# Weight sums of the seven-product pairs made in block zero and split when read; block one on seven products too

## What is computed

```python
h = rmsnorm(x, g_pre)
proj = h @ w_in                       # 1024 x 10240: twelve parts of 512 columns, then 4 x 1024 gate columns
out_a, out_b, out_c, out_d = ...      # chunk mixing | 31-tap conv | pooling | 3-tap conv, each times silu(z)
merged = sum(sigmoid(gate_i + b_i) * (out_i @ w_branch[i]) for i in range(4))
y = merged @ w_out
x = x + rmsnorm(y, g_post)
```

## Time and profile before

| | |
|---|---|
| median of 3 runs | 2377.5 us (2376.88 to 2377.93) |
| profiled execution | 2379.08 us, span 2377.0 us |
| mean granted TensorE clock | 0.998 |
| TensorE matmul busy | 2356.2 us, 99% |
| VectorE, ScalarE, GpSimd busy | 1568.0, 442.9, 633.1 us |
| DMA | 686.63 MB, mean 289 GB/s |

### The profile page before, as it was taken

One profiled execution on the slowest core, in us unless ns is written; L12 is line 12 of the kernel. 1 busy time (PEld: TensorE's weight loads), 2 busy tenths in 40 slices (PEclk: granted clock), 3 DMA queues, 4 the chain that ended last, 5 costly groups with the idle time before them and its releaser, 6 DMA issues.

```text
span 2377.0 us, 34997 instructions
## 1 busy us (share of the span) xinstructions
PE 2356.2 (99%) x13240; PEld 2086.9 (88%) x13240; DVE 1568.0 (66%) x2347; ACT 442.9 (19%) x646; POOL 633.1 (27%) x423
## 2 busy tenths in 40 slices
PE   9999999999999999999999999999999999999998
PEld 7888888888788888788888899999898999999998
DVE  7886887855666577775266866776337776577643
ACT  5223222323112111122101100111110110010111
POOL 4435545455545646656200000000100000000000
PEclk9999999999999999999999999999999999999999
DMA  8977878788998998999765599999875458988884
GB/s 329 321 249 278 308 261 326 271 296 329 376 326 288 364 328 321 371 325 363 292 252 186 204 322 374 306 331 323 271 252 163 157 186 287 332 281 267 282 284 173
DMA packets 286115, 686.63 MB, mean 289 GB/s; under 512 B 19665, under 2 KB 97873, under 8 KB 258577
## 3 DMA queue, kind: packets, MB, share of 16 engines
q1 hardware_dynamic: 273520, 652.18, 78.3%
q10 hardware_dynamic: 12448, 32.49, 3.6%
HBM read 514.14 MB, written 170.46 MB: 288 GB/s over the span
## 4 chain that ended last, share of the span: by engine, by line
PE 88%; DVE 5%; issue 2%; POOL 1%; POOLq 1%; DMA 1%; DVEq 1%; ACT 1%; SPq 0%; ACTq 0%
PE acc L1928 47%; PE acc L2146 18%; PE side L2157 7%; PE side L2072 4%; PE side L2146 4%; PE acc L2306 3%; PE side L2306 3%; POOL s_lo L669 1%; DMA w_pair<-split_main 1%; PE acc L2303 1%; PE side L2303 1%; PE side L2100 1%; PE side L2090 1%; DVE t_sum L1413 0%; PE acc L2336 0%
## 5 line engine op out<-in xcount | busy, mean ns | idle before, releaser
L1928 PE MATMUL acc<-h_hi,w_pair 128*128 128x512 f32 x2752 | 866.2, 390 | 6.4 <-DMA w_pair<-split_main 6.2
L1928 PEld LDWEIGHTS acc<-h_hi,w_pair 128*128 128x128 f32 x2752 | 517.4, 188 | 116.2 <-issue 7.7
L1928 PE MATMUL acc<-h_lo,w_pair 128*128 128x512 f32 x1376 | 536.1, 390 | 0.0
L1200 DVE SCALAR_TENSOR_TENSOR cb<-glu,col,cb 128x512 f32<-128x512 f32 x600 | 425.0, 773 | 18.9 <-issue 10.9
L648 POOL TENSOR_TENSOR w_pair<-w_raw,w_pair 128x1024 fp32r<-128x1024 f32 x118 | 268.4, 2286 | 273.1 <-ACT w_pair L779 258.1
L678 POOL TENSOR_TENSOR rstd<-msq,nhalf 128x5 f32<-128x5 f32 (+4 forms) x19 | 19.9, 1047 | 1126.7 <-DVE msq L1110 532.3
L1928 PEld LDWEIGHTS acc<-h_lo,w_pair 128*128 128x128 f32 x1376 | 258.6, 188 | 53.4
L2146 PE MATMUL acc<-t_hi,chunk 128*128 128x256 f32 (+1 forms) x1344 | 266.8, 287 | 1.3 <-DVE merged L1505 1.3
L2146 PEld LDWEIGHTS acc<-t_hi,chunk 128*128 128x128 f32 x1344 | 216.6, 189 | 2.0 <-DVE merged L1505 1.7
L2146 PE MATMUL acc<-h_hi,chunk 128*128 128x256 f32 (+1 forms) x1008 | 205.1, 289 | 2.6 <-issue 1.5
L2146 PE MATMUL acc<-t_lo,chunk 128*128 128x256 f32 (+1 forms) x672 | 193.0, 287 | 0.0
(11 more groups left out here) (327 smaller groups left out, 3405.6 us busy)
## 6 DMA issues: line engine op xcount, KB each, us to landing
w_pair<-split_main SPq DMA_DIRECT2D x118, 1024.0 KB, 7.2
chunk<-split_main SPq DMA_DIRECT2D x226, 512.0 KB, 5.8
chunk<-s_parts SPq DMA_DIRECT2D x200, 512.0 KB, 6.2
split_main<-w_pair SPq DMA_DIRECT2D x88, 1024.0 KB, 6.7
w_raw<-in_w_main SPq DMA_DIRECT2D x88, 512.0 KB, 5.1
chunk<-split_branch SPq DMA_DIRECT2D x62, 512.0 KB, 4.5
s_raw<-in_w_main SPq DMA_DIRECT2D x100, 256.0 KB, 6.0
s_parts<-s_hi SPq DMA_DIRECT2D x50, 512.0 KB, 5.2
```

What stands on the lines that cost most here:

```text
L1200: dve.scalar_tensor_tensor(dst, src, c1("conv_w", c * CK + t), dst, ALU.mult, ALU.add)
L1928: ins = pe.matmul(acc[:, s, b, 0:m], w_k[:, wt, wk], mv_[:, k, t0:t0 + m], start=(k == 0 and n == 0), stop=(k == nk - 1 and n == 2))
```

## The change

SEVEN0 becomes 1: block one does its 25 pairs with seven products as blocks two and three do. The weight sums are made in block zero by GpSimd, from the raw tiles while both units of a pair lie in the ring, just before the low part of the pair's second unit. A pair's units are f and f + 2 in the G sections (f + 1 and f + 3 are branch tiles) and f and f + 1 in D and Z. The sums are stored unsplit (1 MB for a pair instead of 2) from one buffer, and the raw tile of either unit is held until they are made. When a sum chunk is read, it is 256 KB; ScalarE casts it (chunk_cast) and GpSimd subtracts (chunk_low). The loops of SP and GpSimd over block zero's units are written out. A small buffer for the sample rows (x_dec) is cut in four pieces, since s_sum takes its place.

```diff
-SEVEN0 = 2
+SEVEN0 = 1
+SUM_AT = (1, 2, 3, 5)
@@ SBUF and DRAM
-    s_parts = nc.dram_tensor("s_parts", (NPAIR, P, 2, 4 * WB), F32).ap()
+    chunk_raw = [sb(f"chunk_raw{c}", [P, WB], addr=pair_at + (c * 2 + 1) * WB * 4) for c in range(CHUNKS)]
+    s_parts = nc.dram_tensor("s_parts", (NPAIR, P, 4, WB), F32).ap()
+    s_sum = sb("s_sum", [P, 4, WB], addr=a + 2 * WMAX * 4 + EL * 4)
@@ SP, raw_load(u, src, n)
+            if u >= RING:
                 sp.wait_ge(w_lo_done, u - RING + 1)
+                if u - RING in PAIR_OF:
+                    sp.wait_ge(s_summed, SUM_RANK[PAIR_OF[u - RING]] + 1)
+            sp.dma_start(w_raw[u % RING][:, 0:n], src).then_inc(w_landed[u % RING], 16)
@@ SP, split_store(u)
+            sp.dma_start(dst, src).then_inc(split_stored[u % RING], 16)
+            if second:
+                sp.wait_ge(s_summed, SUM_RANK[p] + 1)
+                sp.dma_start(s_parts[p, :, :, :], s_sum[:, :, :]).then_inc(s_stored, 16)
@@ SP, for every unit u of block zero
+                        raw_load(u, raw_rows(m), DM)
+                if u >= RING:
+                    split_store(u - RING)
@@ SP, blocks after
-                        for h in range(NH):
-                            if HALF_STORE[h] == u // 2:
-                                s_store(h)
...
-                                s_load(h)
+            dst = chunk_raw[n % CHUNKS][:, :] if STREAM[n][0] == "sum" else f(chunk[n % CHUNKS])
+            sp.dma_start(dst, chunk_source(*STREAM[n])).then_inc(chunk_landed[n % CHUNKS], 16)
@@ GpSimd
+        def lo(u, n):
             pool.wait_ge(w_hi_done, u + 1)
+            s, p = u % RING, PAIR_OF.get(u)
+            if p is not None and u == PAIR_UNITS[p][1]:
+                pair_weights(p)
             pool.tensor_tensor(w_lo[s][:, 0:n], w_raw[s][:, 0:n], f(w_hi[s])[:, 0:n],
                                ALU.subtract).then_inc(w_lo_done, 1)
+        def pair_weights(p):
...
+            s1, s2, s3, s4 = (s_sum[:, c, :] for c in range(4))
+            if SUM_RANK[p]:
+                pool.wait_ge(s_stored, 16 * SUM_RANK[p])
+            pool.tensor_tensor(s3, a21, a11, ALU.subtract)
             pool.drain()
+            pool.tensor_tensor(s1, a22, a21, ALU.add)
+            pool.tensor_tensor(s2, a22, s3, ALU.add)
             pool.drain()
+            pool.tensor_tensor(s4, a12, s2, ALU.subtract)
             pool.drain().then_inc(s_summed, 1)
+        def chunk_low(j, p, at):
+
+            n = PAIR_AT[j, p][0] + at
+            pool.wait_ge(c_hi_done, sum_no(j, p, at) + 1)
+            pool.tensor_tensor(chunk[n % CHUNKS][:, 1, :], chunk_raw[n % CHUNKS][:, :], f(chunk[n % CHUNKS])[:, 0, :],
+                               ALU.subtract).then_inc(c_lo_done, 1)
@@ ScalarE
+        def chunk_cast(j, p, at):
+
+            n = PAIR_AT[j, p][0] + at
+            act.wait_ge(chunk_landed[n % CHUNKS], 16 * (n // CHUNKS) + 16)
+            act.activation(chunk[n % CHUNKS][:, 0, :], chunk_raw[n % CHUNKS][:, :], ACT.Copy).then_inc(c_hi_done, 1)
@@ ScalarE, seven_pairs
                 copy_p1(j, p)
+                chunk_cast(j, p, SUM_AT[3])
+                if p + 1 < NPAIR:
+                    chunk_cast(j, p + 1, SUM_AT[0])
+                    chunk_cast(j, p + 1, SUM_AT[1])
+                    if name == "D":
+                        chunk_cast(j, p + 1, SUM_AT[2])
...
+                        if t == 0 and p + 1 < NPAIR:
+                            chunk_cast(j, p + 1, SUM_AT[2])
@@ TensorE, product
+                if summed is None:
+                    landed(n)
+                else:
+                    pe.wait_ge(c_lo_done, summed + 1)
```

More of the change, by code:

```diff
@@ L420, in gp, with sum_no @@
         return (j - SEVEN0) * NPAIR + p
+    def sum_no(j, p, at):
+        return 4 * gp(j, p) + SUM_AT.index(at)
     def chunk_no(j, p):
@@ L572, in s_store @@
-        def s_store(h):
-            q, hx, b = h // 2, h % 2, h % 3
-            sp.wait_ge(s_lo_done, h + 1)
-            for n, part in enumerate((s_hi[b], s_lo[b])):
-                dst = s_parts[q, :, n, :].rearrange("p (c n) -> p c n", c=8)
-                sp.dma_start(dst[:, hx::2, :], f(part)).then_inc(s_stored[b], 16)
+            for r in range(count):
+                u = UNIT0[name] + r
+                if u:
+                    m = unit_pieces(name, r)[0][1]
+                    if name[0] == "G" and r % 2:
+                        raw_load(u, raw_branch_rows(m), WB)
+                    else:
+                        raw_load(u, raw_rows(m), DM)
+                if u >= RING:
+                    split_store(u - RING)
+                if u == RING - 1:
+                    for dst, src in [(bs_bc[:, :, :], bs_rows.partition_broadcast(P)),
+                                     (ws[:, :, :], ws_t), (tmp[:, 0:P], mask_t), (poolw[:, :, :], pool_w),
+                                     (smp_g[:, :, :], st_conv), (smp_c[:, :, :], st_pool), (smp_d[:, :, :], st_short)]:
+                        sp.dma_start(dst, src).then_inc(const_loaded, 16)
@@ L751, in _ @@
+            power(TPB)
+            if last:
+                power(1, DEC)
+            for at in SUM_AT[:3]:
+                chunk_low(j, 0, at)
+            for p, pair in enumerate(PAIRS):
+                chunk_low(j, p, SUM_AT[3])
+                if pair == ("G2", 2) or pair == ("G3", 0) and not last:
+                    power(TPB + 1)
+                if p + 1 < NPAIR:
+                    for at in SUM_AT[:3]:
+                        chunk_low(j, p + 1, at)
             if not last:
@@ L2138, in _, with product @@
             tt = {n: [t_hi[j, n], t_lo[j, n]] for n in range(1, 5)} if is_seven(j) else {}
-            def product(n, rhs, bank):
-                landed(n)
+            def product(n, rhs, bank, summed=None):
+                if summed is None:
+                    landed(n)
+                else:
+                    pe.wait_ge(c_lo_done, summed + 1)
                 wt = chunk[n % CHUNKS]
@@ L2190, in seven_pairs @@
                         pe.wait_ge(pair_summed, 6 * g - 1)
-                    product(n + 1, tt[2], bank[1])
+                    product(n + 1, tt[2], bank[1], sum_no(j, p, 1))
                     if p == 0:
@@ L2196, in seven_pairs @@
                         pe.wait_ge(pair_summed, 6 * g)
-                    product(n + 2, tt[3], bank[2])
+                    product(n + 2, tt[3], bank[2], sum_no(j, p, 2))
                     if name == "G2" and q:
@@ L2211, in seven_pairs @@
                         pe.wait_ge(t_lo_done, 4 * (j - SEVEN0) + 3)
-                    product(n + 3, tt[1], bank[3])
+                    product(n + 3, tt[1], bank[3], sum_no(j, p, 3))
                     pe.wait_ge(p1_copied, g + 1)
@@ L2215, in seven_pairs @@
                     pe.wait_ge(pair_summed, 6 * g + 1)
-                    product(n + 5, h22, bank[1])
+                    product(n + 5, h22, bank[1], sum_no(j, p, 5))
                     pe.wait_ge(pair_summed, 6 * g + 2)
```

224 lines of the change are left out of this document (59 added, 165 removed).

## The result

The change makes the kernel slower: 2524.87 us against 2377.38, both medians of four runs (2522.89 to 2531.49 and 2376.88 to 2377.93), ratio 1.0624 with a 95% interval of 1.0612 to 1.0637. The forecast was 2454 with a range of 2400 to 2505: right in direction, 71 us short, outside the range.

The account below looks back on a forecast made before the run. TensorE was taken to bound the kernel, busy 2356.2 of 2377.0 us. The median 2377.5 − 28.7 (block one) + 100.7 (block zero) + 5 (blocks one to three) gave 2454.5, rounded 2454, range 2400 to 2505.

Parts of the forecast that it names:

- Part 1: Block one: taking the seven products shortens it by 28.7 us, bounds 24 and 30.
- Part 2: Block zero: making and storing the weight sums lets GpSimd's loops set the pace, a loss of 100.7 us.
- ledger of 24 intervals: Block zero, 25 pairs: 12 gate intervals of 18.8 and 12 touching D or Z of 17.7, less TensorE's 337.3 us.
- The store loop: Block zero: one s_sum buffer, so each pair's sums wait for the store before; 17.7 us in D, 17.6 in gates.
- hold loop: Gate sections: split store waits behind the raw load that needs the sums, delaying casts and low parts; 18.8 us a pair.
- PW: GpSimd in block zero: four sum operations of 1.5 us plus 0.24 for drains, 6.2 us a pair, bounds 5.4 and 7.2.
- after the long ones only: TensorE in block zero: its clock would be reduced only after long waits, 6 to 7 us in D.
- Part 3: Blocks one to three: chunk casts fit, GpSimd's new work slows VectorE and delays TensorE, +5 us, bounds 0 and +30.
- Long landings: Rival in block zero: stores queue and VectorE slows GpSimd, D and gates 20, loss 143, 2497 us; chance 0.14.
- late chunk chain: Rival in blocks one to three: new casts stall each pair by 1 us, 2529 us; chance 0.06.
- Short landings: Rival in block zero: stores land in 5.2 us, D 15.4, gates 17.6, loss 59, 2413 us; chance 0.24.
- faster side: Rival in block zero: stores hardly matter, GpSimd's plain pace decides, D loses 5 us, 2359 us; chance 0.06.

Follow-up runs that it names:

- run 11: Changed kernel with SP's raw loads ahead of the sum store, x_half loaded early, and GpSimd's low part of sum chunks cut to 8 columns: 2406.5 us.
- run 4: Changed kernel with only the first pair's sums stored and read by all pairs, the other 24 stores and their waits left out: 2468.2 us.
- run 1: Changed kernel with SP issuing the sum store right after the raw load that waits for the sums, ahead of the split stores: 2495.7 us.
- run 2: Changed kernel with SP issuing a unit's split store before the raw load that waits for the sums: 2474.6 us.
- run 3: Changed kernel with both the early sum store and the split store ahead of the raw load on SP: 2469.9 us.
- run 8: Changed kernel with GpSimd issuing the sum store on its own queue, and the split store first on SP: 2481.5 us.
- run 10: Changed kernel with SP issuing split stores, then raw loads, then the sum store, and x_half loaded early: 2454.41 us, ratio 1.0316 to the kernel before.
- run 5: Changed kernel with GpSimd's low part of sum chunks cut to 8 of 512 columns, products taking the high part instead: 2490.5 us.
- run 9: Changed kernel with ScalarE issuing the x_half load ahead of the casts of the first G2 pair: 2528.8 us.
- run 12: Changed kernel with SP's raw loads ahead of the sum store, x_half's load left behind the casts: 2452.8 us.
- run 7: Changed kernel with the four sum operations cut to 8 of 512 columns, the stores kept: 2424.2 us.

## Why the prediction was right in direction and wrong in size

**Part 1 is right.** Block one in run 11 takes 557.4, 27.4 less than before (forecast 28.7). Seven products do free that time; the change itself keeps 9.8 of it.

**Part 2: loops right, sizes short.** From the first pair's sums (188.67) to the last's (657.69) is 469.0 us; TensorE's work in it was put at 337.3. Loss 131.7, which is block zero's +130.1. So the ledger of 24 intervals holds, and there was no reserve before it. The 12 gate intervals sum to 244.6, 20.4 each instead of 18.8, and the 12 with D or Z to 224.4, 18.7 instead of 17.7. That is 19 and 12 us.

The step that failed is "The store loop gives 17.6 there and is hidden by this one". Measured, that loop is the longer: sums 6.4 (417.66 to 424.06), 5.72 until the store starts, 8.21 to land, 20.3 with the sums again. The medians over the gate pairs say the same: 6.1 for the sums, 5.7 until the store starts, 8.4 until the next sums. The forecast let the sum store start 3.9 us after the sums (2.65 for the low part, 0.17, and two issues of 0.53), with rows from a queue of one raw load and one store; in the burst of the gates the issues before it take 1.2 to 1.5 us each. And it took a landing of 7.5 where 8.2 was to come. The hold loop was sized nearly right, 19.5 measured alone in run 4 against 18.8, and ends second. PW came out well, 6.1 us at the median against 6.2, though no row stood behind its 0.24 us for the drains: after, the three drains leave 0.14, 0.14 and 0.18 us idle, as in the interval shown above. Two loops of nearly the same length also tell why no single reordering wins it all back: runs 1 to 3, 8 and 10 shorten one loop and meet the next. In D the forecast of 17.7 met 18.1 (the same three terms: 6.1, 4.3 and 7.8). A misreading stood in the forecast: the second unit's split store carries only the columns from 512 on, 512 KB and not 1 MB; that form lands in 7.0 us at the median against 6.7 for the 1 MB one. So in D the sum store follows 1 MB and not 1.5; what that is worth no run shows.

TensorE waited 4.1 to 6.0 us a pair in D (forecast 6 to 7) and mostly 1.4 to 2.7 in the gates (2 to 3). The clock fell after more waits than the forecast's "after the long ones only": the first matmul took 0.76 to 0.80 us after 16 waits, among them five of 2.3 to 2.7 us in the gates, and 0.47 to 0.50 after five others of 1.4 to 4.7 us. From 290 to 380 us the granted clock was 0.87, from 400 to 500 us it was 0.90. As forecast, that costs nothing of its own while GpSimd's loop is the longer: the 24 intervals alone account for the loss, 131.7 against 130.1.

**Part 3 failed: "Taken +5 us for three blocks; bounds 0 and +30"**, measured 42.8. The sign named for it, a block over 10 us longer than block two was, is there in blocks one and two (18.9 and 15.3). The mechanism named in it, GpSimd slowing VectorE, is right: taking it away gives 30 us in run 5, and with the early x_half in run 11 nearly all. The failing term is its price, 5 us. The share was taken for the merge additions, which hardly slow down in the pairs (min/median/max, VectorE after):

```profile
L1526 DVE TENSOR_TENSOR merged<-merged,tmp x24: 691/692/1137, 1043.2 to 1251.7; 128x512 f32<-128x512 f32 x24
```

The conv step pays instead, 64 × 0.3 = 20 us in block one, and others with it: VectorE is busy 1728.8 us after and 1608.4 in run 5, so 120 us come from the subtractions. That this "nearly fills" VectorE was read, and then priced by what remains free on average; the waits come at single banks, 12 for zc and 3 for the side bank, while VectorE over the whole of block two is busy only 401 of 571 us. The second price missing, put at nothing without a reason, was the x_half load in ScalarE's queue: a DMA issued behind instructions that wait for a transfer. By run 11 against 5 it holds 12 us back. Since runs 9 and 12 show nothing for it with full low parts, the two do not add; they overlap.

**The rivals.** Long landings, 2497 with gates 20 and D 20, had the right gates and the wrong D, and lacked the 38 us of part 3. The late chunk chain came to 2529, by chance near the result: TensorE waited for GpSimd's chunks 1.5 us in all. Short landings would need 5.2 us; the least of 25 was 7.2. The faster side is excluded: with the stores gone (run 4) block zero still loses 71, and with the sums nearly gone (run 7) 29, as much as part 1 gives at the most.

**Still open.** What sets the gates' 18.4 us in run 10, with occasional intervals of 22 (ScalarE waits there 20 times for a raw load to land, 57.8 us in all, but no run takes that away); what makes VectorE late in block zero of run 4; and whether the 42.8 us could be had back by moving low parts to another engine, which was not tried. No version here beats the kernel before; in D the floor of this plan is that GpSimd needs 12.0 us for a pair and TensorE 10.88.

## What to carry to other kernels

When a buffer is made, stored and made again, lay out the whole loop with the queue as it will be after the change: count every issue ahead of the store in its burst, and price the issues by a burst, not by a lone pair. Before giving an idle GpSimd new work, look for VectorE instructions that slow down beside it, form by form, and ask which TensorE bank waits on them; a share of busy time hides this. A DMA issued from a compute engine's queue inherits each wait put ahead of it.

## What the hardware showed

**Of some pairs of VectorE and GpSimd instructions, the one that began second waits for the other.** After, GpSimd's timeline and then VectorE's in block one:

```profile
1154.35 2.55 POOL L648 TENSOR_TENSOR chunk<-chunk_raw,chunk 128x512 fp32r<-128x512 f32 x2 [5.31 <-ACT chunk L738]
1157.90 1.30 POOL L648 TENSOR_TENSOR chunk<-chunk_raw,chunk 128x512 fp32r<-128x512 f32 x1 [1.01 <-ACT chunk L738]
```
```profile
1154.37 0.42 DVE L1505 TENSOR_TENSOR zc<-acc,zc 128x256 f32<-128x256 f32 x1 [0.25 <-PE acc L2099]
1155.68 0.42 DVE L1507 TENSOR_TENSOR zc<-acc,zc 128x256 f32<-128x256 f32 x1 [0.89 <-PE acc L2099]
1156.03 1.15 DVE L1601 TENSOR_SCALAR cb<-cb,col 128x512 f32<-128x512 f32 x1
...
1157.87 1.62 DVE L1601 TENSOR_SCALAR cb<-cb,col 128x512 f32<-128x512 f32 x1
...
1162.51 0.53 DVE L1601 TENSOR_SCALAR cb<-cb,col 128x512 f32<-128x512 f32 x1
```

GpSimd ends at 1156.90 and 1159.20; the two scalings end 0.28 and 0.29 later, at 1.15 and 1.62 us instead of 0.53. The additions with a PSUM operand, at 1154.37 and 1155.68, keep their 0.42 beside the same GpSimd work. The conv step's 737/747/1827 is the same picture. Of the 128 in the pairs of blocks one and two, 48 take 0.92 us or more, and each of these ends 0.55 us after one of GpSimd's subtractions does. Fourteen of the others began before the subtraction that runs beside them, and kept their 0.75; there the subtraction is the longer one, 1.81 us where it began 0.09 us after VectorE's and 1.29 where it began 0.61 after. One of the 48, GpSimd first and then VectorE:

```profile
1029.60 1.42 POOL L648 TENSOR_TENSOR chunk<-chunk_raw,chunk 128x512 fp32r<-128x512 f32 x1 [3.12 <-ACT chunk L738]
```
```profile
1029.96 1.60 DVE L1151 SCALAR_TENSOR_TENSOR cb<-glu,col,cb 128x512 f32<-128x512 f32 x1
```

The Trainium skill (SBUF — State Buffer, SBUF: two separate sides) says that the two engines share a pair of SBUF ports as an exclusive lock, held for a whole instruction by whichever starts first, and that a VectorE instruction needs it when it runs in a two-port mode or has two SBUF inputs. The trace agrees for the conv step, by the 0.55 us. The scaling has one SBUF tensor and is held up as well; whether it ran in a two-port mode no run here shows.

**An issue on SP costs 0.33 us at the head of a burst and up to 2.1 later in one** (run 3, 1.85 of it shown at 401.16), seven in a row 6.6 us.

**A sum store of 1 MB lands in 6.5 to 8.2 us at the median**, by the order of issue: 8.2 behind the burst (after), 6.5 early (run 1), 6.8 from GpSimd's queue (run 8).
